# Values of a decoder's attention layer as seven block products between the heads, with two weight sums on GpSimd

## The chip, the core and the metric

The kernel runs on one core of one Trainium2 chip, in one launch. The metric is device time in microseconds of that core. TensorE (PE) multiplies, VectorE (DVE), ScalarE (ACT) and GpSimd (POOL) work element by element, SyncE (SP) issues most DMAs. Each engine takes its own instructions in the order of its program, and the engines meet at semaphores.

## The reference, cut to what matters

A two-layer decoder trunk on 256 tokens of width 1024, all in float32. Layer 0 is a recurrent block with a mixture of experts; layer 1 is causal attention with a mixture of experts. Keys and values come from the residual stream once, queries from the layer's input:

```python
h = layer_norm(xs, g, b)
kv = (h @ w_kv).reshape(B, S, 2, N_HEADS, HEAD_DIM)      # 256x1024 @ 1024x2048
k = apply_partial_rope(kv[:, :, 0], cos, sin)
v = kv[:, :, 1]
q = apply_partial_rope((x @ w_q).reshape(B, S, N_HEADS, HEAD_DIM), cos, sin) * (HEAD_DIM ** -0.5)
...                                                      # MOBA_BLOCK = SEQ = 256: plain causal attention
probs = jax.nn.softmax(s_own, axis=-1)                   # 8 heads of 128, 256 queries x 256 keys
out = probs @ v_own
return out.reshape(B, S, N_HEADS * HEAD_DIM) @ w_o
```

What matters here is v = h @ w_v, a product of 256x1024 by 1024x1024, and the eight heads that are worked on beside it.

## The kernel before, in words

The program is written out by hand for each engine, and a wait is a wait for a count of a semaphore. Layer 1's attention runs through these steps:

- Keys and queries (`keys0`, `query0`) are each formed as seven block products in place of eight: the tokens are split in two (c) and the inner and the output dimension in halves (j, h). The blocks are combined beforehand by four sums of weights (t1 to t4, each 128x2048) and four sums of operands (s1 to s4, each 128x512) on DVE, and afterwards by sums over the products in PSUM. `first_sum`, `second_sum`, `third_sum`, `fourth_sum` make t1 to t4, `kq_operands` makes s1, s2, s4, s3, `middle_products` and `kq_last` multiply, `middle_sums`, `seventh_sums` and `last_sum` combine. `sums_at` numbers all these sums on the one semaphore `sums`.
- `heads(c, b, count)` turns (transposes) a half of the tokens by heads behind `rope`; `heads_out` copies the result out of PSUM on ACT and DVE.
- Values are plain: `values_in(h, c, ks)` (L1043) multiplies one of four output blocks over eight chunks k, 32 products of 128x512, and `values_out` (L1316) copies a block to `vt` on ACT.
- Of head h, `head_scores(h)` (L1047) multiplies queries by keys; DVE takes the row maxima (L2028 to L2030, `negmax`); `exped(h)` on ACT (L1344) exponentiates; `probs(h)` on DVE (L2018) divides by the sum, in place in `prob`; `head_turn(h)` on PE (L1057) turns the probabilities; `turned(h)` on ACT (L1354) copies them to one of four places of `prT`; `head_values(h)` on PE (L1067) multiplies them by the values; `heads_done(j)` on ACT (L1360) copies two heads' output to `oT`.
- PE's order (L1078 to L1117) puts pieces of the values between the heads: two products of 128x512 stand between the scores of a head and the turning of the head before it. `head_values` 0 to 2 lie among them, 3 behind `head_turn(6)`, 4 to 7 behind `head_turn(7)`.
- DVE's order (L1985 to L2034): the sums of keys and queries, then `weight_sums(1)` (L1447: two sums of 128x2048 for the output projection `mix(1)`), the last `heads_out`, and then nothing but maxima and probabilities till the last head. After that `moe(1)` begins with `operand_sums(1)` for the output projection.
- `mix(1)` (L631) multiplies `oT` by the output weights, again with seven products; the routing and the experts follow. SP issues the loads of experts 3 and 5 of layer 1 when the values are multiplied (L546), that of expert 4 behind the last head (L549), those of experts 0 and 1 behind the output projection (L551), and in a loop the rest (`expert_loop`).
- GpSimd clears six small tiles at the start (L1397 to L1404) and does nothing else.

The line of most matmuls in the profile is that of the helper `mm`, L564; turning a half by heads is L670, turning probabilities L1064, all ACT operations L1125, sums over PSUM on DVE L1529.

Of the kernel before, what the change touches and what calls it, by code (L numbers as in the profile page):

```python
# [100 lines left out]
SEVEN = ("mix0", "pg0", "keys0", "query0", "mix1", "pg1")  # L101
# [4 lines left out]
FIRST_OUT = {"mix0": 1, "pg0": 2, "keys0": 5, "query0": 6, "mix1": 9, "pg1": 10}  # L106
# [7 lines left out]
FAR = 3e38  # L114

# [22 lines left out]
def build(nc, xt_d, x_d, pt_d, cst_d, cstb_d, chan_d, rows_d, tab_d, win_d, gates_d, wout_d, shared_d,  # L138
          router_d, experts_d, ple_d, pgate_d, wkv_d, wq_d, wo_d, out_d):
    ctx = ExitStack()  # L140
    with ctx:
# [97 lines left out]
        prT = z[:, :, :].rearrange("p c n -> p (c n)")[:, 0:4 * 3 * P].rearrange("p (b n) -> p b n", b=4)  # L239
# [114 lines left out]
        KQ_BANK = {"keys0": {"A": 0, "C": 1, "B": 2, "D": 3, "last": 2}, "query0": {"A": 4, "C": 5, "B": 6, "D": 7, "last": 6}}  # L354
        KQ_NAME = {"keys0": "wk", "query0": "wq"}
        KQ_MM = {"keys0": "k_mm", "query0": "q_mm"}
        KQ_SUM = {"keys0": (3, 11), "query0": (7, 11)}
        KQ_JOINT = {"keys0": joint, "query0": flat[:, 3 * D:3 * D + HALF]}

        def kq_lhs(stage, c, j):  # L360
            return {"keys0": hkT, "query0": xT}[stage][:, 4 * j:4 * j + 4, own(c)]
# [35 lines left out]
        def _(sp):  # L397
# [148 lines left out]
            sp.wait_ge(S("v_mm"), TC * 2)  # L546
# [15 lines left out]
        def _(pe):  # L562
# [7 lines left out]
            pe.wait_ge(S("pads0"), 1)  # L570
# [388 lines left out]
            def project(lhs, name, c, h, b, done, ks=range(KC)):  # L959

                for k in ks:
                    m = mm(bank(b), lhs[:, k, own(c)], kmajor(f"{name}{k // 2}")[:, k % 2, half(h)], k == 0, k == KC - 1)
                if KC - 1 in ks:
                    m.then_inc(S(done), 1)

# [25 lines left out]
            def middle_products(stage):  # L991
# [5 lines left out]
                kq_product(stage, "C", GSUM[0], kq_sum(stage, 0))  # L997
# [4 lines left out]
                kq_product(stage, "B", GSUM[1], kq_sum(stage, 1))  # L1002
                pe.wait_ge(S("first_out"), {"keys0": 7, "query0": 8}[stage])
                pe.wait_ge(S("sums"), sums_at[stage, "s4"])
                kq_product(stage, "C", GSUM[3], kq_weight(stage, 1, 1), False)
                pe.wait_ge(S("sums"), sums_at[stage, "t3"])
                pe.wait_ge(S("sums"), sums_at[stage, "s3"])
                kq_product(stage, "D", GSUM[2], kq_weight(stage, 0, 1))

            def kq_last(stage):  # L1010

                pe.wait_ge(S("sums"), sums_at[stage, "t4"])
                kq_product(stage, "last", kq_lhs(stage, 1, 1), kq_weight(stage, 0, 0))
# [29 lines left out]
            def values_in(h, c, ks):  # L1043

                project(hkT, "wv", c, h, 2 * h + c, "v_mm", ks)
# [21 lines left out]
            def head_values(h):  # L1067

                b, o = (h // 2) % 2, (h % 2) * T
                pe.wait_ge(S("v_out"), 2 if h < 4 else 4)  # L1070
# [3 lines left out]
                mm(PS[:, b, o:o + T], vt[:, 0, h * P:h * P + P], prT[:, h % 4, 0:T], True, False, True)  # L1074
                mm(PS[:, b, o + P:o + T], vt[:, 1, h * P:h * P + P], prT[:, h % 4, T:3 * P], False, True, True
                   ).then_inc(S("value_mm"), 1)
# [5 lines left out]
            values_in(0, 0, range(KC))  # L1082
            heads(1, 6, 8)
            values_in(0, 1, range(0, 2))
# [38 lines left out]
        def _(act):  # L1123
# [174 lines left out]
            def second_out(stage):  # L1298

                act.wait_ge(S(KQ_MM[stage]), 2)  # L1300
                out, src = tokm[:, 0, half(0)], PS[:, KQ_BANK[stage]["A"], :]
                if stage == "keys0":
                    out, src = out.rearrange("p (b t) -> p b t", b=2), PS[:, 0:2, 0:T]
                a(out, src, ACT.Copy).then_inc(S("copied"), 1)

            def third_out(stage):

                act.wait_ge(S(KQ_MM[stage]), 3)
                a(tokm[:, 1, half(1)], PS[:, KQ_BANK[stage]["C"], :], ACT.Copy).then_inc(S("first_out"), 1)

# [4 lines left out]

            def values_out(n, h, c):  # L1316

                act.wait_ge(S("v_mm"), n)
                a(vt[:, c, half(h)], PS[:, 2 * h + c, :], ACT.Copy).then_inc(S("v_out"), 1)
# [21 lines left out]
            values_out(1, 0, 0)  # L1341
# [12 lines left out]
            def turned(h):  # L1354
                act.wait_ge(S("probT_mm"), h + 1)
                if h >= 4:
                    act.wait_ge(S("value_mm"), h - 3)
                a(prT[:, h % 4, :], PS[:, 6 + h % 2, 0:3 * P], ACT.Copy).then_inc(S("probT_out"), 1)
# [6 lines left out]
            exped(0)  # L1365
            exped(1)
            turned(0)
            exped(2)
            values_out(2, 0, 1)
# [8 lines left out]
            values_out(3, 1, 0)  # L1378
            heads_done(0)
            turned(5)  # L1380
            exped(7)
            load_norm(2)
            turned(6)
# [11 lines left out]
        @block.gpsimd  # L1395
        def _(pool):
            nc.gpsimd.memset(z[:, 0, 0:T], 0.0).then_inc(S("pads0"), 1)  # L1397
            nc.gpsimd.memset(pads[:, :, 0:3], 0.0).then_inc(S("pads0"), 1)
            nc.gpsimd.memset(eps[:, :], LN_EPS).then_inc(S("pads0"), 1)
            nc.gpsimd.memset(onesr[:, :], 1.0).then_inc(S("pads0"), 1)  # L1400
            nc.gpsimd.memset(rankt[:, :, NOBLK:NCOL], -AWAY).then_inc(S("pads0"), 1)
            nc.gpsimd.memset(gtmp[:, :, 0, 4:NG], FAR).then_inc(S("pads0"), 1)
            pool.wait_ge(S("pads0"), 6)
            nc.gpsimd.memset(ovs[:, 2:4], 0.0).then_inc(zero_ok, 1)  # L1404


        @block.vector
        def _(dve):
# [439 lines left out]
            def kq_operands(stage, steps):  # L1848

                a11, a21, a12, a22 = (kq_lhs(stage, c, j) for j in range(2) for c in range(2))  # L1850
                for i in steps:
                    if i:
                        dve.wait_ge(S("sums"), sums_at[stage, ("s1", "s2")[min(i, 2) - 1]])
                    out, x, y, op = ((GSUM[0], a21, a22, ALU.add), (GSUM[1], GSUM[0], a11, ALU.subtract),
                                     (GSUM[3], a12, GSUM[1], ALU.subtract), (GSUM[2], a11, a21, ALU.subtract))[i]
# [103 lines left out]
            def middle_sums(stage):  # L1959

                dve.wait_ge(S(KQ_MM[stage]), 4)
                dve.wait_ge(S("first_out"), {"keys0": 7, "query0": 8}[stage])
                own_joint, banks = KQ_JOINT[stage], KQ_BANK[stage]
                step(added(own_joint, own_joint, PS[:, banks["B"], :]))
                step(added(tokm[:, 1, half(1)], tokm[:, 1, half(1)], own_joint))
                dve.wait_ge(S(KQ_MM[stage]), 5)
                step(added(tokm[:, 0, half(1)], own_joint, PS[:, banks["C"], :]))

            def seventh_sums(stage):

                dve.wait_ge(S(KQ_MM[stage]), 6)
                step(added(tokm[:, 1, half(1)], tokm[:, 1, half(1)], PS[:, KQ_BANK[stage]["D"], :]))
                step(added(tokm[:, 1, half(0)], KQ_JOINT[stage], PS[:, KQ_BANK[stage]["D"], :]))

            def last_sum(stage):

                dve.wait_ge(S(KQ_MM[stage]), KQ)
                step(added(tokm[:, 1, half(0)], tokm[:, 1, half(0)], PS[:, KQ_BANK[stage]["last"], :]))
# [36 lines left out]
            weight_sums(1)  # L2015
            heads_out(8, qT, 1, 7, "heads_dve")

# [7 lines left out]
            for i in range(NH + 1):  # L2025
# [5 lines left out]
                if i >= 1:  # L2031
                    probs(i - 1)
            n = moe(1)
# [115 lines left out]
```

## Time and profile before

| what | value |
|---|---|
| time, median of 3 runs | 1233.07 us (1232.51 to 1233.27) |
| the profiled execution | 1231.53 us, span 1229.7 us |
| PE busy | 1177.7 us, 96% of the span |
| DVE busy | 496.2 us, 40% |
| ACT busy | 260.5 us, 21% |
| POOL busy | 1.0 us |
| mean granted TensorE clock | 0.983 |

The profile's page has the busy time by engine, a strip of 40 slices, the chain of work that ended last, and the costliest groups of instructions. The trace behind it can be asked for the instructions of a stretch in order of time (the timeline), for busy time and granted clock by stretch (the windows), and for who waited for whom. All times in a stretch are microseconds from the start of the span. Spans of one timeline row overlap a little with the next, since the ends of matmuls are modelled: the time from start to start is what a group takes.

### The profile page before, as it was taken

To read this page: it belongs to the slowest core of one execution; us is meant where nothing else is said; L and a number is where in the kernel's file an instruction comes from. 1 tells how busy PE (TensorE), PEld (TensorE's weight loads), DVE (VectorE), ACT (ScalarE), POOL (GpSimd) and SP (SyncE) were. 2 spreads that over 40 slices of the span, in tenths; PEclk is the share of its full clock that TensorE was granted. 3 is DMA by queue.
4 is the path that set the end of the run, shared out by engine and by line. 5 is a ranking of instruction groups with operands and counts; after the bars stand their busy time and mean duration, and the time that the engine had idled before them with its cause. 6 is when DMAs were issued, how large, how long until landed. Compare 5 with 4: busy or idle time off the path is not lost.

```text
span 1229.7 us, 15413 instructions
## 1 busy us (share of the span) xinstructions
PE 1177.7 (96%) x5908; PEld 597.9 (49%) x5908; DVE 496.2 (40%) x1172; ACT 260.5 (21%) x471; POOL 1.0 (0%) x11
## 2 busy tenths in 40 slices
PE   9999997969999999999999999997599999999998
PEld 7866443425444444444645555442244444444344
DVE  4787432122222223226885383322122233223147
ACT  1513111101111112112412422120112111122112
POOL 0000000000000000000000000000000000000000
PEclk9999999979999999999999999998799999999999
DMA  9966999999999999999635478999999999999990
GB/s 379 400 244 284 403 420 419 427 425 428 424 425 426 424 426 425 419 421 421 274 137 205 165 321 339 414 417 424 426 425 426 425 424 425 425 424 423 421 401 36
DMA packets 50475, 461.65 MB, mean 375 GB/s; under 512 B 5729, under 2 KB 6242, under 8 KB 9186
## 3 DMA queue, kind: packets, MB, share of 16 engines
q1 hardware_dynamic: 48816, 456.09, 89.1%
q10 hardware_dynamic: 1586, 4.57, 1.0%
q8 instruction: 47, 0.77, 0.3%
q14 instruction: 26, 0.21, 0.0%
HBM read 459.60 MB, written 1.05 MB: 375 GB/s over the span
## 4 chain that ended last, share of the span: by engine, by line
PE 86%; DMA 8%; issue 3%; SPq 2%; DVE 1%; ACTq 0%; DVEq 0%
PE ps L564 82%; DMA weights<-in_experts 7%; SPq L406 2%; PE ps L670 1%; PE ps L843 1%; PE ps L850 1%; DMA xT<-in_xt 1%; SPq L409 1%; DVE x_lo L1611 0%; PE ps L1064 0%; SPq L456 0%; DVE x_res L1789 0%; DVE z L1788 0%; DVE onehot L1619 0%; DVE scratch L1699 0%
## 5 line engine op out<-in xcount | busy, mean ns | idle before, releaser
L564 PE MATMUL ps<-weights,xT 128*64 128x512 f32 (+2 forms) x1912 | 463.9, 605 | 43.0 <-issue 37.8
L564 PE MATMUL ps<-weights,scratch 128*64 128x512 f32 (+3 forms) x1192 | 328.1, 590 | 1.3 <-DVE scratch L1699 1.2
L564 PEld LDWEIGHTS ps<-weights,xT 128*64 128x64 f32 (+2 forms) x1912 | 151.7, 135 | 290.3 <-issue 277.9
L564 PEld LDWEIGHTS ps<-weights,scratch 128*64 128x64 f32 (+2 forms) x1192 | 114.4, 144 | 145.8 <-issue 143.5
L564 PE MATMUL ps<-scratch,xT 128*64 128x512 f32 (+2 forms) x384 | 158.1, 566 | 0.1
L1696 DVE TENSOR_TENSOR scratch<-scratch,ps 128x256 f32<-128x256 f32 x56 | 23.6, 421 | 314.1 <-ACT scratch L1125 314.1
L1709 DVE SCALAR_TENSOR_TENSOR y_lo<-ps,slot_weight,y_hi 128x512 fp32r<-128x512 f32 x112 | 84.0, 751 | 152.6 <-ACT y_hi L1125 152.6
L1125 ACT ACTIVATE y_hi<-ps,slot_weight 128x512 fp32r<-128x512 f32 x112 | 76.7, 687 | 251.6 <-PE ps L564 238.8
L1125 ACT ACTIVATE scratch<-ps 128x256 f32<-128x256 f32 (+2 forms) x75 | 30.5, 406 | 459.4 <-PE ps L564 442.4
L1125 ACT ACTIVATE xT<-ps 128x512 f32<-128x512 f32 x132 | 77.5, 598 | 97.9 <-PE ps L564 82.6
L564 PE MATMUL ps<-onehot,x_hi 128*128 128x256 f32 x448 | 91.1, 289 | 0.0
L564 PE MATMUL ps<-onehot,x_lo 128*128 128x256 f32 x448 | 89.0, 283 | 0.5 <-DVE x_lo L1611 0.3
L564 PEld LDWEIGHTS ps<-onehot,x_hi 128*128 128x128 f32 x448 | 69.8, 189 | 24.6 <-issue 21.3
L564 PE MATMUL ps<-y_hi,onehot_T 128*128 128x512 f32 x224 | 80.6, 438 | 0.0
L564 PE MATMUL ps<-scratch 128*64 128x512 f32 (+1 forms) x160 | 72.8, 598 | 0.0
L564 PEld LDWEIGHTS ps<-scratch,xT 128*64 128x64 f32 (+2 forms) x384 | 49.6, 143 | 47.0 <-issue 45.1
L1699 DVE COPY scratch<-ps 128x256 f32<-128x256 f32 x56 | 23.8, 425 | 120.5 <-PE ps L843 120.5
L564 PE MATMUL ps<-y_lo,onehot_T 128*128 128x512 f32 x224 | 70.8, 394 | 0.0
L564 PEld LDWEIGHTS ps<-onehot,x_lo 128*128 128x128 f32 x448 | 68.8, 190 | 1.3 <-DVE x_lo L1611 1.3
L564 PE MATMUL ps<-xT,weights 128*128 128x256 f32 x256 | 56.4, 380 | 1.6 <-DMA xT<-in_xt 1.5
L564 PEld LDWEIGHTS ps<-xT,weights 128*128 128x128 f32 x256 | 48.4, 190 | 9.3 <-DMA xT<-in_xt 2.8
L564 PEld LDWEIGHTS ps<-y_hi,onehot_T 128*128 128x128 f32 x224 | 34.5, 190 | 25.5 <-issue 23.7
(210 smaller groups left out, 769.7 us busy)
## 6 DMA issues: line engine op xcount, KB each, us to landing
weights<-in_experts SPq DMA_DIRECT2D x90, 2048.0 KB, 19.4
weights<-in_experts SPq DMA_DIRECT2D x140, 1024.0 KB, 24.4
scratch<-in_experts SPq DMA_DIRECT2D x18, 2048.0 KB, 20.9
scratch<-in_experts SPq DMA_DIRECT2D x24, 1024.0 KB, 22.0
weights<-in_pgate SPq DMA_DIRECT2D x8, 1024.0 KB, 27.2
weights<-in_wkv SPq DMA_DIRECT2D x8, 1024.0 KB, 26.2
weights<-in_win SPq DMA_DIRECT2D x7, 1024.0 KB, 20.0
weights<-in_shared SPq DMA_DIRECT2D x6, 1024.0 KB, 10.4
```

Of the source, the lines that this page charges most:

```text
L406: sp.dma_start(E(SLOT_OF[p])[:, ks], src[:, ks]).then_inc(S(f"{GATE_UP[part]}{p // 2 % 4}_loaded_{L}"), 16)
L409: sp.dma_start(E(SLOT_OF[p])[:, GU:EXPERT], src[:, GU:EXPERT]).then_inc(S(f"down{p // 2 % 4}_loaded_{L}"), 16)
L564: return nc.tensor.matmul(out, lhsT, rhs, start=first, stop=last, skip_group_check=shared_bank)
L670: m = nc.tensor.transpose(PS[:, b + j, k * P:k * P + P], src[:, c, (4 * j + k) * P:(4 * j + k + 1) * P], ident)
L843: m = nc.tensor.transpose(PS[:, 6, f * P:f * P + P], hh[:, f * P:f * P + P], ident)
L850: m = nc.tensor.transpose(PS[:, 7, (2 + c) * P:(3 + c) * P], ohw[:, c, :], ident)
L1125: return nc.scalar.activation(out, in_, f, **kw)
L1696: v.tensor_tensor(hh, sg, PS[:, 6, DE:2 * DE], ALU.mult).then_inc(S(f"hidden_{L}"), 1)
L1699: v.tensor_copy(hT.rearrange("p f s -> p (f s)"), PS[:, 6, 0:DE]).then_inc(S(f"hidT_{L}"), 1)
L1709: v.scalar_tensor_tensor(y_lo[:, half(h)], PS[:, 4 + h, :], wslot[:, 0:1], y_hi[:, half(h)].bitcast(F32), ALU.mult, ALU.subtract).then_inc ...
```

## The change

- Values become a third stage, `value0`, of the seven block products: 28 products of 128x512 in place of 32. The first of them is `value_part` (two halves into one bank), then `first_sum_product`, `second_sum_product`, `fourth_sum_product`, `third_sum_product`, `kq_last`, one each between the scores of one head and the turning of the head before.
- `value0` needs four sums of weights. t1 and t2 are made on DVE, t1 where `weight_sums(1)` was, t2 behind the last `heads_out` and two operand sums. t3 and t4 are made on GpSimd, which waits for t1, and for t2 and the first product. t1 waits for all of `query0`'s products, since it is written over query weights.
- The operand sums s1 and s2 stand on DVE behind the last `heads_out`, s4 and s3 behind head 0's maxima; the sums over the products (`middle_sums`, `seventh_sums`, `last_sum`) behind the probabilities of heads 2, 3 and 4. Two of the four output blocks are copied on ACT (`second_out`, `third_out`), the other two are written by DVE.
- `head_values` moves: 0 and 1 behind `head_scores(6)`, with no product between, 2 behind `head_scores(7)`, 3 to 5 behind `head_turn(6)`, 6 and 7 behind `head_turn(7)`. `prT` has five places in place of four. On ACT, `heads_done(0)` and `heads_done(1)` stand behind `turned(6)`.
- `weight_sums(1)` moves behind the last probabilities. The router weights' load on ACT's queue moves ahead of `turned(6)`. SP's load of experts 3 and 5 waits for the seventh product.

```diff
+HEADS_AHEAD = 5
...
+                   "value0": {"A": 0, "C": 1, "B": 2, "D": 3, "last": 2}}
+        KQ_SUM = {"keys0": (3, 11), "query0": (7, 11), "value0": (0, 1)}
+        VSUM = [xT[:, 2 * i:2 * i + 2, :].rearrange("p k s -> p (k s)").rearrange("p (k s) -> p k s", k=4) for i in range(4)]
...
-            sp.wait_ge(S("v_mm"), TC * 2)
+            sp.wait_ge(S("v_mm"), KQ)
...
+            def third_sum_product(stage):
+
+                if stage == "value0":
+                    pe.wait_ge(S("pool_sums"), 7)
+                else:
+                    pe.wait_ge(S("sums"), sums_at[stage, "t3"])
                 pe.wait_ge(S("sums"), sums_at[stage, "s3"])
...
-            values_in(0, 0, range(KC))
+            value_part(0, range(4))
             heads(1, 6, 8)
-            values_in(0, 1, range(0, 2))
+            pe.wait_ge(S("first_out"), FIRST_OUT["value0"])
+            value_part(1, range(0, 2))
...
             head_scores(0)
-            values_in(0, 1, range(2, 4))
+            value_part(1, range(2, 4))
             head_scores(1)
-            values_in(0, 1, range(4, 6))
+            first_sum_product("value0")
             head_turn(0)
             head_scores(2)
-            values_in(0, 1, range(6, 8))
+            second_sum_product("value0")
             head_turn(1)
             head_scores(3)
-            values_in(1, 0, range(0, 2))
+            fourth_sum_product("value0")
             head_turn(2)
             head_scores(4)
-            values_in(1, 0, range(2, 4))
+            third_sum_product("value0")
             head_turn(3)
             head_scores(5)
-            head_values(0)
-            values_in(1, 0, range(4, 6))
+            kq_last("value0")
             head_turn(4)
             head_scores(6)
+            head_values(0)
             head_values(1)
-            values_in(1, 0, range(6, 8))
             head_turn(5)
             head_scores(7)
             head_values(2)
-            values_in(1, 1, range(0, 4))
             head_turn(6)
-            values_in(1, 1, range(4, 8))
             head_values(3)
+            head_values(4)
+            head_values(5)
             head_turn(7)
-            for h in range(4, NH):
-                head_values(h)
+            head_values(6)
+            head_values(7)
...
             exped(0)
+            second_out("value0")
             exped(1)
+            third_out("value0")
             turned(0)
...
-            values_out(4, 1, 1)
-            act.dma_start(routw, router_d).then_inc(S("router_loaded"), 16)
+            heads_done(0)
+            heads_done(1)
             turned(7)
-            for j in range(1, 4):
-                heads_done(j)
+            heads_done(2)
+            heads_done(3)
...
+            for i in range(4):
+                arrived(pool, f"wv{i}")
+            pool.wait_ge(S("sums"), sums_at["value0", "t1"])
+            nc.gpsimd.tensor_tensor(kq_weight("value0", 0, 1), kq_weight("value0", 1, 1), kq_weight("value0", 0, 1), ALU.subtract
+                                    ).then_inc(S("pool_sums"), 1)
+            pool.wait_ge(S("v_mm"), 1)
+            pool.wait_ge(S("sums"), sums_at["value0", "t2"])
+            nc.gpsimd.tensor_tensor(kq_weight("value0", 0, 0), kq_weight("value0", 1, 0), kq_sum("value0", 1), ALU.subtract
+                                    ).then_inc(S("pool_sums"), 1)
...
             rope(7, 1, 0)
-            weight_sums(1)
+            first_sum("value0")
             heads_out(8, qT, 1, 7, "heads_dve")
+            kq_operands("value0", range(0, 2))
+            second_sum("value0")
...
                 if i >= 1:
                     probs(i - 1)
+                if i == 0:
+                    kq_operands("value0", range(2, 4))
+                elif i == 3:
+                    middle_sums("value0")
+                elif i == 4:
+                    seventh_sums("value0")
+                elif i == 5:
+                    last_sum("value0")
+            weight_sums(1)
             n = moe(1)
```

## Rows read from the trace of the kernel before

**Rows 1.** The page: busy us, share of the span, instructions, by engine.

```profile
PE 1177.7 (96%) x5908; PEld 597.9 (49%) x5908; DVE 496.2 (40%) x1172; ACT 260.5 (21%) x471; POOL 1.0 (0%) x11
```

**Rows 2.** Windows: stretch, its length, busy us by engine, clock, DMA.

```profile
665.00:700.00 35.00, 35.00 (x151) 21.39 (x151) 11.38 (x48) 15.24 (x48) 0.00 (x0) 1.00 0.18 61
700.00:735.00 35.00, 34.97 (x130) 19.49 (x129) 28.09 (x71) 10.25 (x16) 0.00 (x0) 1.00 0.81 336
```

**Rows 3.** Timeline of PE, values and heads: start, us, engine, line, operation.

```profile
656.21 7.03 PE L564 MATMUL ps<-weights,scratch 128*128 128x512 f32 x16
663.08 1.04 PE L670 MATMUL ps<-cst,z 128*128 128x128 f32 x8
...
672.03 1.94 PE L564 MATMUL ps<-weights,scratch 128*128 128x512 f32 x4
673.80 0.51 PE L1064 MATMUL ps<-cst,scratch 128*128 128x128 f32 x3
674.14 0.39 PE L564 MATMUL ps<-scratch,lnp 128*128 128x128 f32 x2
...
674.97 1.94 PE L564 MATMUL ps<-weights,scratch 128*128 128x512 f32 x4
...
688.01 0.87 PE L564 MATMUL ps<-z,scratch 128*128 128x256 f32 x4
688.72 3.60 PE L564 MATMUL ps<-weights,scratch 128*128 128x512 f32 x8
692.15 0.49 PE L1064 MATMUL ps<-cst,scratch 128*128 128x128 f32 x3
...
696.90 2.87 PE L564 MATMUL ps<-z,scratch 128*128 128x256 f32 x16
699.60 3.60 PE L564 MATMUL ps<-weights,xT 128*128 128x512 f32 x8
```

**Rows 4.** Timeline of DVE, the same stretch.

```profile
636.31 0.69 DVE L1856 TENSOR_TENSOR scratch<-scratch,xT 128x512 f32<-128x512 f32 x1
...
657.94 2.29 DVE L1453 TENSOR_TENSOR weights<-weights 128x2048 f32<-128x2048 f32 x1
...
664.15 0.69 DVE L1983 COPY lnp<-ps 128x512 f32<-128x512 f32 x1 [1.50 <-PE ps L670]
...
672.23 0.29 DVE L2028 TENSOR_REDUCE wgtt<-ps 128x1 f32<-128x128 f32 x1 [1.46 <-PE ps L564]
...
673.16 0.29 DVE L2021 TENSOR_SCALAR scratch<-scratch,wgtt 128x128 f32<-128x128 f32 x1
673.36 0.35 DVE L2022 TENSOR_SCALAR scratch<-scratch,wgtt 128x256 f32<-128x256 f32 x1
...
700.43 0.69 DVE L1529 TENSOR_TENSOR scratch<-xT 128x512 f32<-128x512 f32 x1 [9.66 <-ACT xT L1125]
```

**Rows 5.** Timeline of ACT, the last turned head and two heads' output.

```profile
697.10 0.49 ACT L1125 ACTIVATE z<-ps 128x384 f32<-128x384 f32 x1 [0.38 <-PE ps L1064]
697.48 0.59 ACT L1125 ACTIVATE xT<-ps 128x512 f32<-128x512 f32 x1
```

**Rows 6.** Timeline of POOL, its two longest instructions of eleven.

```profile
0.71 0.31 POOL L1397 MEMSET z<- 128x256 f32 x1 [0.29 <-POOLq L2139]
...
1.04 0.26 POOL L1400 MEMSET ones_row<- 128x192 f32 x1
```

**Rows 7.** Timeline of PE behind its longest idle time.

```profile
882.84 1.07 PE L564 MATMUL ps<-weights,xT 128*32 128x512 f32 x2 [12.59 <-issue]
...
888.78 0.59 PE L564 MATMUL ps<-scratch,xT 128*32 128x512 f32 x1
...
889.21 0.59 PE L564 MATMUL ps<-scratch,xT 128*32 128x512 f32 x1
```

**Rows 8.** Windows over and behind that idle time, columns as in rows 2.

```profile
870.00:883.00 13.00, 0.41 (x6) 0.19 (x8) 2.44 (x10) 0.69 (x1) 0.00 (x0) 0.70 1.00 425
883.00:886.00 3.00, 3.00 (x16) 0.71 (x15) 0.00 (x0) 0.00 (x0) 0.00 (x0) 0.50 1.04 437
```

**Rows 9.** Timeline of SP: loads of experts around the output projection.

```profile
724.73 0.33 SPq L402 DMA_DIRECT2D weights<-in_experts  x1
...
742.76 2.52 SPq L406 DMA_DIRECT2D weights<-in_experts  x4
```

More of the change, by code:

```diff
@@ L353, in build @@
         KQ = 7
[L354 to L358, printed above, removed]
+        KQ_BANK = {"keys0": {"A": 0, "C": 1, "B": 2, "D": 3, "last": 2}, "query0": {"A": 4, "C": 5, "B": 6, "D": 7, "last": 6},
+                   "value0": {"A": 0, "C": 1, "B": 2, "D": 3, "last": 2}}
+        KQ_NAME = {"keys0": "wk", "query0": "wq", "value0": "wv"}
+        KQ_MM = {"keys0": "k_mm", "query0": "q_mm", "value0": "v_mm"}
+        KQ_SUM = {"keys0": (3, 11), "query0": (7, 11), "value0": (0, 1)}
+        KQ_JOINT = {"keys0": joint, "query0": flat[:, 3 * D:3 * D + HALF], "value0": joint}
+        KQ_OUT = {"keys0": tokm, "query0": tokm, "value0": vt}
+        VSUM = [xT[:, 2 * i:2 * i + 2, :].rearrange("p k s -> p (k s)").rearrange("p (k s) -> p k s", k=4) for i in range(4)]
+        KQ_OPERANDS = {"keys0": GSUM, "query0": GSUM, "value0": VSUM}
         def kq_lhs(stage, c, j):
-            return {"keys0": hkT, "query0": xT}[stage][:, 4 * j:4 * j + 4, own(c)]
+            return {"keys0": hkT, "query0": xT, "value0": hkT}[stage][:, 4 * j:4 * j + 4, own(c)]
         def kq_weight(stage, j, h):
@@ L956, in _ @@
             after(0)
[L959 to L964, printed above, removed]
             def heads(c, b, count):
@@ L1041, in _, with value_part @@
             kq_last("query0")
-            def values_in(h, c, ks):
-                project(hkT, "wv", c, h, 2 * h + c, "v_mm", ks)
+            def value_part(j, ks):
+                for k in ks:
+                    m = mm(bank(KQ_BANK["value0"]["A"]), kq_lhs("value0", 0, j)[:, k, :], kq_weight("value0", j, 0)[:, k // 2, k % 2, :],
+                           j == 0 and k == 0, k == 3, j == 1)
+                if 3 in ks:
+                    m.then_inc(S("v_mm"), 1)
             def head_scores(h):
@@ L1069, in head_values @@
                 b, o = (h // 2) % 2, (h % 2) * T
-                pe.wait_ge(S("v_out"), 2 if h < 4 else 4)
+                pe.wait_ge(S("v_out"), 2)
                 pe.wait_ge(S("probT_out"), h + 1)
@@ L1300, in second_out @@
                 act.wait_ge(S(KQ_MM[stage]), 2)
-                out, src = tokm[:, 0, half(0)], PS[:, KQ_BANK[stage]["A"], :]
+                out, src = KQ_OUT[stage][:, 0, half(0)], PS[:, KQ_BANK[stage]["A"], :]
                 if stage == "keys0":
                     out, src = out.rearrange("p (b t) -> p b t", b=2), PS[:, 0:2, 0:T]
-                a(out, src, ACT.Copy).then_inc(S("copied"), 1)
+                a(out, src, ACT.Copy).then_inc(S("v_out" if stage == "value0" else "copied"), 1)
             def third_out(stage):
                 act.wait_ge(S(KQ_MM[stage]), 3)
-                a(tokm[:, 1, half(1)], PS[:, KQ_BANK[stage]["C"], :], ACT.Copy).then_inc(S("first_out"), 1)
+                a(KQ_OUT[stage][:, 1, half(1)], PS[:, KQ_BANK[stage]["C"], :], ACT.Copy).then_inc(S("first_out"), 1)
             def heads_out(n, dst, c, b, done):
@@ L1355, in turned @@
                 act.wait_ge(S("probT_mm"), h + 1)
-                if h >= 4:
-                    act.wait_ge(S("value_mm"), h - 3)
-                a(prT[:, h % 4, :], PS[:, 6 + h % 2, 0:3 * P], ACT.Copy).then_inc(S("probT_out"), 1)
+                if h >= HEADS_AHEAD:
+                    act.wait_ge(S("value_mm"), h - HEADS_AHEAD + 1)
+                a(prT[:, h % HEADS_AHEAD, :], PS[:, 6 + h % 2, 0:3 * P], ACT.Copy).then_inc(S("probT_out"), 1)
             def heads_done(j):
@@ L1377, in _ @@
             exped(6)
-            values_out(3, 1, 0)
-            heads_done(0)
             turned(5)
@@ L1853, in kq_operands @@
                         dve.wait_ge(S("sums"), sums_at[stage, ("s1", "s2")[min(i, 2) - 1]])
-                    out, x, y, op = ((GSUM[0], a21, a22, ALU.add), (GSUM[1], GSUM[0], a11, ALU.subtract),
-                                     (GSUM[3], a12, GSUM[1], ALU.subtract), (GSUM[2], a11, a21, ALU.subtract))[i]
+                    sums = KQ_OPERANDS[stage]
+                    out, x, y, op = ((sums[0], a21, a22, ALU.add), (sums[1], sums[0], a11, ALU.subtract),
+                                     (sums[3], a12, sums[1], ALU.subtract), (sums[2], a11, a21, ALU.subtract))[i]
                     v.tensor_tensor(out, x, y, op).then_inc(S("sums"), 1)
@@ L1961, in middle_sums @@
                 dve.wait_ge(S(KQ_MM[stage]), 4)
-                dve.wait_ge(S("first_out"), {"keys0": 7, "query0": 8}[stage])
+                dve.wait_ge(S("first_out"), THIRD_OUT[stage])
                 own_joint, banks = KQ_JOINT[stage], KQ_BANK[stage]
                 step(added(own_joint, own_joint, PS[:, banks["B"], :]))
-                step(added(tokm[:, 1, half(1)], tokm[:, 1, half(1)], own_joint))
+                step(added(KQ_OUT[stage][:, 1, half(1)], KQ_OUT[stage][:, 1, half(1)], own_joint))
                 dve.wait_ge(S(KQ_MM[stage]), 5)
-                step(added(tokm[:, 0, half(1)], own_joint, PS[:, banks["C"], :]))
+                step(added(KQ_OUT[stage][:, 0, half(1)], own_joint, PS[:, banks["C"], :]))
             def seventh_sums(stage):
                 dve.wait_ge(S(KQ_MM[stage]), 6)
-                step(added(tokm[:, 1, half(1)], tokm[:, 1, half(1)], PS[:, KQ_BANK[stage]["D"], :]))
-                step(added(tokm[:, 1, half(0)], KQ_JOINT[stage], PS[:, KQ_BANK[stage]["D"], :]))
+                step(added(KQ_OUT[stage][:, 1, half(1)], KQ_OUT[stage][:, 1, half(1)], PS[:, KQ_BANK[stage]["D"], :]))
+                step(added(KQ_OUT[stage][:, 1, half(0)], KQ_JOINT[stage], PS[:, KQ_BANK[stage]["D"], :]))
             def last_sum(stage):
                 dve.wait_ge(S(KQ_MM[stage]), KQ)
-                step(added(tokm[:, 1, half(0)], tokm[:, 1, half(0)], PS[:, KQ_BANK[stage]["last"], :]))
+                ins = added(KQ_OUT[stage][:, 1, half(0)], KQ_OUT[stage][:, 1, half(0)], PS[:, KQ_BANK[stage]["last"], :])
+                if stage == "value0":
+                    ins.then_inc(S("v_out"), 1)
+                else:
+                    step(ins)
             def heads_out(n, dst, c, b, done):
```

62 lines of the change are left out of this document (36 added, 26 removed), and 3 rows, old and new, of the table SUM_ORDER.

## The prediction

> **What bounds the kernel now.** I read the page's shares first: PE is busy 96% of the span, DVE 40%, POOL not at all [rows 1]. Then the windows of the stretch that the change touches, 665 to 700 and on to 735: PE busy 35.00 of 35.00 us and 34.97 of 35.00, at full granted clock, DVE busy 11.38 us and DMA at 0.18 in the first [rows 2]. So PE's own list sets the time there, and anything that makes PE stand still is added one for one. Last I read the timelines of PE, DVE and ACT, to see how far ahead of PE each waited-for step is done [rows 3 to 5]. That distance is small: the scores of a head are through at 672.03, the turning of the head before starts at 673.80, 1.77 us later [rows 3]. Two products in between take 1.72 us, so 0.05 us is already waited for.
>
> Does a shift of PE at 700 reach the end? The experts' stream is bound by DMA (PE stands still while the DMA share is 1.00, [rows 8]), but it is started by PE: experts 0 and 1 are issued at 724.73, behind the output projection, and the first of the loop at 742.76 [rows 9]. Both move with PE. The earlier issue of experts 3 and 5 only fills a stretch in which DMA waits for PE anyway. I pass shifts on in full.
>
> **Removed.** A product of 128x512 is two instructions, and 16 instructions take 663.08 - 656.21 = 6.87 us, 0.429 us each [rows 3]. 28 products in place of 32 take away eight: **-3.44 us**. The four waits of 0.05 us in front of head_turn(0) to (3) go as well, since a whole product block (3.43 us) now stands where 1.72 us stood: **-0.2 us**.
>
> **The tail of the heads.** From the scores to the turned head a path of 1.77 us must pass: 0.20 us until DVE starts at 672.23, maxima and probabilities until 673.36 + 0.35 = 673.71, 0.09 us until PE starts [rows 3, 4]. What stands beside it now?
> - head_turn(5) stands behind head_scores(6) and two head_values. One of these takes 688.72 - 688.01 = 0.71 us [rows 3], two 1.42: PE waits **0.35 us**.
> - head_turn(6) stands behind head_scores(7) and one head_values: 1.77 - 0.71 = **1.06 us**.
> - head_values(4) needs heads_done(0), which ACT now does behind turned(6). After the turning: 0.20 us until ACT starts, turned 0.38 us until the next, the copy 0.59 (start to start, and length, [rows 5]), 0.1 until PE: 1.3 to 1.4 us, of which head_values(3) covers 0.71: **0.66 us**.
> - head_turn(7) is far enough back. head_values(7) no longer stands behind three others (in the before four take 2.70 us, [rows 3]), but its copy is covered by head_values(6) up to about **0.1 us**.
>
> Together +2.2 us. With the two terms above the change stands at 2.2 - 3.44 - 0.2 = **-1.5 us** if nothing else stops PE.
>
> **DVE's new work, by itself.** The head of the list, replayed from rows: t1 657.94 to 660.23 (as before), PE is done with the first block at 656.21 + 3.44 and with the turning 0.87 us later at 660.5, heads_out from 660.7, s1 from 661.3 (0.69 us and 0.04 of link each, [rows 4]), s2 from 662.1, t2 from 662.7 to 665.0, the maxima of head 0 from 664.9 although its scores are there at 663.1, s4 and s3 0.6 us each, probabilities of head 0 done at 668.4. PE reaches head_turn(0) at 669.1, behind its third block. Nothing is late; the slack is **0.6 us**. Later heads have 3.44 us beside a path of 1.77, against at most two or three extra sums of 0.73 us, which fall where DVE waited (middle_sums and seventh_sums wait for PE's blocks, and the maxima queued behind them are late by at most 0.3 us). weight_sums(1) took the slot from 657.94; now it runs behind the last probabilities in DVE's idle 9.66 us before 700.43 [rows 4], and is done about when heads_done(3) is. The output projection's second product needs it 3.4 us after the first starts: cost nothing. If that cover were gone, each would cost 2.29 us.
>
> **GpSimd's two sums.** No row of the trace shows such an instruction, nor GpSimd and DVE at work together. Its length g: at least DVE's 2.29 us for the same shape [rows 4]; from above, its memsets grow by 0.05 us from 192 to 256 elements, 0.8 us per 1000 [rows 6], and a sum touches 3 x 2048 elements: 5.1 us. Two accesses instead of three would be 3.4. I take 4.3, the middle of the last two, being GpSimd's own rows. PE wants t3 behind its sixth block, near 680, and t4 20 us later than t2: their length costs PE nothing directly. What they do to DVE is the open cost. Below, zero: both work undisturbed. Above: a DVE operation that uses SBUF on both inputs, or runs at two elements a cycle (tensor_scalar, 0.06 us more for 128 more elements, [rows 4]), stands until the GpSimd instruction is through.
>
> In that case: GpSimd starts t3 at 660.3, DVE's s1 stands from 661.3 to 660.3 + g. t2 follows 3.7 us later and ends at 664.0 + g. At once GpSimd starts t4, and after the maxima of head 0 DVE stands again, until 664.1 + 2g. Behind this are queued s4, s3, the maxima of head 1 and the probabilities of head 0, 2.8 us, and on PE head_turn(0) with everything after it: it starts at 667.0 + 2g in place of 669.1. PE's wait is **2g - 2.1 us**: 6.5 us at g = 4.3, 2.5 at 2.3, 8.1 at 5.1. The change as a whole is then 2g - 3.6, zero at g = 1.8.
>
> I take the upper end of this cost, at g = 4.3: **+6.5 us**, sum **+5.0 us**. The rows by themselves don't decide between the ends; I hold that two engines reading four streams of SBUF at once exclude each other to be likelier than that they don't.
>
> The Trainium skill speaks against this change here. "SBUF — State Buffer", section "SBUF: two separate sides", says that DVE and GpSimd take turns at a shared pair of ports, as an exclusive lock held for a whole instruction, for DVE operations with two SBUF inputs among others; by it the wait is the full one, and without it the change would be -1.5 us. "GPSIMD Engine Reference", section "3.1 Elementwise — side-by-side cycle accounting", gives 4497 ns for a sum of 2048 float32 elements beside 2293 ns on DVE; the trace agrees on DVE's (2.29 us), no row shows GpSimd's, and with it the sum, as an estimate, would be 5.4 in place of 5.0 us.
>
> **The clock.** With 6.5 us of standing, PE's clock may fall. Over its idle 12.59 us before 882.84 the granted clock averages 0.70, and it is 0.50 (1.2 GHz) in the 3 us behind it [rows 7, 8]. From 882.84 to 888.78 seven rounds of four matmuls take 5.94 us; the next takes 0.43 [rows 7], so 5.94 - 7 x 0.43 = 2.9 us were lost. No row shows a wait as short as ours: between 0 and 2.9 us. Of the rows with any fall this is the only kind, and I take **+2.9 us**.
>
> **Sum.** -3.44 - 0.2 + 2.2 + 6.5 + 2.9 = +7.9 us on the profiled span of 1229.7: 1237.6, an execution of 1239.5. The profiled execution (1231.53) is 1.5 us below the median, and I add the difference to the median: **1241.0 us**.
>
> **Rivals.**
> - Full block, as above: 1236.5 to 1243.5, according to g and the clock. Chance 0.58.
> - No contention: DVE runs at full rate beside GpSimd, PE waits only in the tail: 1231.6 us. For it: nothing in the rows forbids it. Chance 0.22; 0.03 of it below 1230.6.
> - Partial contention: DVE's operations are stretched, not stopped, and half of the block's delay is seen: 1233.1 - 1.5 + 3.3 = 1234.9. It decides at the 0.6 us of slack in front of head_turn(0). Chance 0.12, half of it over 1235.5.
> - **The other side:** no contention, and the tail's waits are not there either, because PE's turning starts earlier than I think behind an idle PE and ACT finds time for heads_done(0) before turned(6) is due. Place: head_turn(6), whose path would have to be 0.71 us instead of 1.77. 1233.1 - 3.6 = 1229.4. Against it: the path of 1.77 us appears four times in the trace. Chance 0.05.
> - weight_sums(1), now behind the last probabilities, is stopped too or late and delays the output projection by one sum and more: 1243 and up. Chance 0.03.
>
> This kernel's measurement can tell about 0.2%, 2.5 us, from no change. Faster (below 1230.6): 0.08; within: 0.25; slower (above 1235.5): 0.67. Range 1230.8 to 1243.5: it takes in the case without contention down to its middle's lower side, and leaves out some 0.17.
>
> **What would show it.** After: PE busy without a gap up to the third block of values, then an idle time of 2g - 2.1 us before L1064's first turning, released by DVE; on DVE gaps before s1 and before s4 that end with a POOL instruction; on POOL two instructions of 4 to 5 us; a granted clock of 0.5 behind the gap; waits of 0.35, 1.06 and 0.66 us in the tail. 56 instructions of value products. What would make it wrong: s1 starting at 661.3 beside a running GpSimd, or GpSimd's sums far shorter or longer than 4.3 us.

## The result and the profile after

The changed kernel takes 1239.77 us (median of 4 runs, 1238.01 to 1241.21), the kernel before 1232.79 us (4 runs, 1232.05 to 1233.27). The ratio is 1.0064, 95% interval 1.005 to 1.0077: slower by 7.0 us. The profiled execution took 1239.84 us, its span is 1238.0 us. Forecast were 1241.0 us in a range of 1230.8 to 1243.5.

The page's first lines and part of its strip, kernel after; they answer to [rows 1]:

```profile
span 1238.0 us, 15424 instructions
PE 1175.7 (95%) x5900; PEld 597.5 (48%) x5900; DVE 514.2 (42%) x1184; ACT 259.7 (21%) x470; POOL 10.0 (1%) x13
PEclk9999998979999999999998999998799999999999
```

PE is busy 2.0 us less, and the kernel is slower all the same. POOL has 9 us of work that it did not have. The timeline of PE, kernel after (start, us, engine, line, operation, and in brackets the idle time and what ended it), answers to [rows 3]:

```profile
666.37 3.65 PE L571 MATMUL ps<-weights,xT 128*128 128x512 f32 x8
676.33 0.90 PE L1090 MATMUL ps<-cst,scratch 128*128 128x128 f32 x3 [6.30 <-DVE scratch L2063]
...
682.76 0.49 PE L1090 MATMUL ps<-cst,scratch 128*128 128x128 f32 x3
...
697.83 1.53 PE L571 MATMUL ps<-z,scratch 128*128 128x256 f32 x8
699.56 0.55 PE L1090 MATMUL ps<-cst,scratch 128*128 128x128 f32 x3 [0.21 <-DVE scratch L2063]
...
700.77 0.87 PE L571 MATMUL ps<-z,scratch 128*128 128x256 f32 x4
702.51 0.55 PE L1090 MATMUL ps<-cst,scratch 128*128 128x128 f32 x3 [0.86 <-DVE scratch L2063]
702.89 0.82 PE L571 MATMUL ps<-z,scratch 128*128 128x256 f32 x4
704.22 1.55 PE L571 MATMUL ps<-z,scratch 128*128 128x256 f32 x8 [0.51 <-ACT xT L1151]
...
707.49 3.60 PE L571 MATMUL ps<-weights,xT 128*128 128x512 f32 x8
```

The third block of values begins at 666.37 and takes eight instructions of 0.429 us, to 669.80. The first turning (L1090, the line that was L1064) starts at 676.33: 6.53 us of standing. Three small waits follow in the tail. The timelines of POOL and DVE, kernel after, show whom PE waits for, and answer to [rows 4] and [rows 6]:

```profile
661.03 4.51 POOL L1431 TENSOR_TENSOR weights<-weights 128x2048 f32<-128x2048 f32 x1 [659.50 <-DVE weights L1857]
669.17 4.49 POOL L1435 TENSOR_TENSOR weights<-weights 128x2048 f32<-128x2048 f32 x1 [3.62 <-DVE weights L1867]
```

```profile
661.36 0.69 DVE L2022 COPY lnp<-ps 128x512 f32<-128x512 f32 x1 [0.49 <-PE ps L677]
661.97 4.13 DVE L1891 TENSOR_TENSOR xT<-scratch 128x512 f32<-128x512 f32 x1
666.13 0.69 DVE L1891 TENSOR_TENSOR xT<-xT,scratch 128x512 f32<-128x512 f32 x1
...
669.14 0.41 DVE L2070 TENSOR_REDUCE wgtt<-ps 128x1 f32<-128x256 f32 x1
669.59 4.10 DVE L2071 TENSOR_SCALAR wgtt<-wgtt 128x2 f32<-128x2 f32 x1
```

The sum s1 is a 128x512 operation like its neighbour s2 of 0.69 us, but its record lasts 4.13; the scaling of two numbers a row, 0.17 us for every other head, lasts 4.10. Less their own length both end 0.13 us before GpSimd's record does (665.41 and 665.54, 673.52 and 673.66). Two instructions that read PSUM run at their usual length beside GpSimd: the copy at 661.36 (0.69 us) and the second of head 0's maxima at 669.14 (0.41 us). The stopped time shows as busy in DVE's row of the page, so its share says nothing of it.

### The profile page after: what moved, and what is told of

Read it like the earlier page. It is cut to its first block, busy times and chain, and to the rows that moved or that the text cites. A ratio compares the mean times of both kernels' runs of the same rounds, so it can differ in the third digit from the quotient of the medians.

```text
span 1238.0 us, 15424 instructions
## 1 busy us (share of the span) xinstructions
PE 1175.7 (95%) x5900; PEld 597.5 (48%) x5900; DVE 514.2 (42%) x1184; ACT 259.7 (21%) x470; POOL 10.0 (1%) x13
## 4 chain that ended last, share of the span: by engine, by line
PE 81%; DMA 9%; SPq 4%; issue 4%; DVE 2%; ACT 0%; ACTq 0%; DVEq 0%
PE ps L571 77%; DMA weights<-in_experts 9%; SPq L413 3%; PE ps L677 1%; PE ps L850 1%; PE ps L857 1%; SPq L416 1%; DMA xT<-in_xt 0%; DVE xT L1891 0%; DVE wgtt L2071 0%; DVE x_lo L1643 0%; PE ps L1090 0%; DVE weights L1867 0%; SPq L463 0%; DVE x_res L1821 0%
## 5 line engine op out<-in xcount | busy, mean ns | idle before, releaser
L571 PE MATMUL ps<-weights,xT 128*64 128x512 f32 (+2 forms) x1944 | 478.5, 603 | 45.3 <-issue 39.8
L571 PE MATMUL ps<-weights,scratch 128*64 128x512 f32 (+3 forms) x1152 | 309.7, 590 | 1.3 <-DVE scratch L1731 1.2
L571 PEld LDWEIGHTS ps<-weights,xT 128*64 128x64 f32 (+2 forms) x1944 | 157.6, 136 | 298.6 <-issue 283.9
L571 PEld LDWEIGHTS ps<-weights,scratch 128*64 128x64 f32 (+2 forms) x1152 | 107.3, 142 | 139.3 <-issue 137.3
L571 PEld LDWEIGHTS ps<-y_lo,onehot_T 128*128 128x128 f32 x224 | 42.0, 188 | 10.1 <-issue 0.5
```

The source lines that it names most:

```text
L571: return nc.tensor.matmul(out, lhsT, rhs, start=first, stop=last, skip_group_check=shared_bank)
```

## The experiments

The theory: a running GpSimd sum stops DVE's next instruction that needs SBUF twice, for as long as it runs; PE waits what exceeds the slack; the tail's waits come from the new order alone. The rivals: DVE's longer list by itself makes PE wait; or the tail's waits are a consequence of the delay at the head. Medians are given with the ratio to the kernel before, run on the same chip.

**e1: all sums on DVE.**

```diff
-            nc.gpsimd.tensor_tensor(kq_weight("value0", 0, 1), kq_weight("value0", 1, 1), kq_weight("value0", 0, 1), ALU.subtract
-                                    ).then_inc(S("pool_sums"), 1)
...
-            nc.gpsimd.tensor_tensor(kq_weight("value0", 0, 0), kq_weight("value0", 1, 0), kq_sum("value0", 1), ALU.subtract
-                                    ).then_inc(S("pool_sums"), 1)
...
+                elif i == 1:
+                    third_sum("value0")
+                elif i == 2:
+                    fourth_sum("value0")
                 elif i == 3:
                     middle_sums("value0")
```

> The changed kernel with t3 and t4 made by DVE (behind the probabilities of heads 0 and 1) instead of GpSimd; all else as changed. Theory (GpSimd's sums hold DVE up): DVE's s1 runs right behind heads_out(8), the 6.5 us of PE standing before head_turn(0) and the half clock behind it are gone, the tail's waits of 0.3, 1.0 and 0.6 us stay; 1.5 us faster than the kernel before, about 1231.4 us. Rival (the longer list of DVE alone, t2 ahead of head 0's maxima, makes PE wait): with two more sums of 2.3 us on DVE it is no faster than the changed kernel, 1239 us or more.

1231.39 us (11 runs), ratio 0.9992, interval 0.9983 to 1.0001. PE's timeline, e1: the standing time is gone, 665.69 + 3.43 = 669.12 to 669.18.

```profile
665.69 3.65 PE L571 MATMUL ps<-weights,xT 128*128 128x512 f32 x8
669.18 0.49 PE L1084 MATMUL ps<-cst,scratch 128*128 128x128 f32 x3
...
673.82 0.38 PE L1084 MATMUL ps<-cst,scratch 128*128 128x128 f32 x2
...
690.62 0.55 PE L1084 MATMUL ps<-cst,scratch 128*128 128x128 f32 x3 [0.21 <-DVE scratch L2048]
693.56 0.55 PE L1084 MATMUL ps<-cst,scratch 128*128 128x128 f32 x3 [0.86 <-DVE scratch L2048]
695.27 1.55 PE L571 MATMUL ps<-z,scratch 128*128 128x256 f32 x8 [0.51 <-ACT xT L1145]
...
698.54 3.60 PE L571 MATMUL ps<-weights,xT 128*128 128x512 f32 x8
```

The interval takes in 1, so e1 is not told apart from the kernel before. DVE has 4.6 us more work than in the changed kernel, and the median is 8.4 us lower: the longer list is not the cause. The three waits of the tail are the same to the hundredth, so they do not come from the delay at the head.

**e2: e1, and another order in the tail.** `last_part` is the last product, one half at a time.

```diff
-            kq_last("value0")
+            last_part(range(0, 2))
             head_turn(4)
             head_scores(6)
-            head_values(0)
-            head_values(1)
+            last_part(range(2, 4))
             head_turn(5)
             head_scores(7)
+            head_values(0)
+            head_values(1)
             head_values(2)
             head_turn(6)
...
-            turned(6)
             heads_done(0)
+            turned(6)
...
-                elif i == 5:
+                elif i == 6:
                     last_sum("value0")
```

> As e1, and the tail put in another order: the last product in two halves in front of head_turn(4) and head_turn(5), head_values 0 to 2 in front of head_turn(6), heads_done(0) ahead of turned(6), last_sum one head later. Theory (the tail's waits are the 1.77 us path with too little beside it): waits of 0.05 us at head_turn(4) and (5), none at head_turn(6) and head_values(4); the whole saving of four products is left, 3.4 us faster than before, about 1229.4 us. Rival (the tail's waits move to the next place, since DVE or ACT is late in sum): the waits appear at other turnings and the time stays at e1's 1231.4 us.

1229.36 us (9 runs), ratio 0.9978, interval 0.9968 to 0.9988: faster than both kernels, and 3.0 us below the kernel before on the same chip (1232.34), where 3.4 had been expected. PE's timeline, e2, has no bracket left in the stretch:

```profile
683.03 1.94 PE L571 MATMUL ps<-weights,scratch 128*128 128x512 f32 x4
685.06 0.55 PE L1094 MATMUL ps<-cst,scratch 128*128 128x128 f32 x3
...
689.21 2.18 PE L571 MATMUL ps<-z,scratch 128*128 128x256 f32 x12
...
695.41 3.60 PE L571 MATMUL ps<-weights,xT 128*128 128x512 f32 x8
```

From e1 to e2 the stretch from the first block of values to the output projection shrinks from 698.54 - 656.17 = 42.37 us to 695.41 - 654.95 = 40.46, by 1.91; the medians differ by 2.03. Where e2 misses its forecast: head_turn(4) starts 2.03 us behind 683.03, not 1.77. DVE's timeline shows why: the two sums of `seventh_sums` (1.41 us, from 682.08) end at 683.5, and the maxima of head 5, ready at 683.2, stand behind them. So 0.26 us of waiting are left there. No bracket shows them, since the modelled end of the products (683.03 + 1.94 = 684.97) lies only 0.09 us ahead of the turning.

**e3: t3 on GpSimd, t4 on DVE** (e1's edit for t4 alone).

> The changed kernel with t3 on GpSimd and t4 on DVE. Theory (each GpSimd sum stops DVE once, for its own length): s1 stands until GpSimd's 4.5 us are over, 3.5 us late, 0.6 of it is slack: PE waits 2.9 us in front of head_turn(0); the change is +1.4 us against before, 1234.2 us, up to 1236 if the clock falls. If what stopped DVE was something else than the running GpSimd instruction, PE's wait stays near 6.5 us.

1234.80 us (7 runs), ratio 1.0023, interval 1.0011 to 1.0035. PE's timeline, e3:

```profile
666.68 3.65 PE L571 MATMUL ps<-weights,xT 128*128 128x512 f32 x8
672.71 0.55 PE L1087 MATMUL ps<-cst,scratch 128*128 128x128 f32 x3 [2.38 <-DVE scratch L2056]
```

From 666.68 + 3.43 = 670.11 to 672.71 are 2.60 us. s1's record is 4.13 us again (3.44 too many), the scaling's 0.17. The wait is 0.3 us shorter than expected.

**e4: both GpSimd sums over half of their columns.** t3 and t4 are formed for the first 256 of 512 columns only, so the kernel does not compute the reference's values.

```diff
...
-            nc.gpsimd.tensor_tensor(kq_weight("value0", 0, 0), kq_weight("value0", 1, 0), kq_sum("value0", 1), ALU.subtract
+            nc.gpsimd.tensor_tensor(kq_weight("value0", 0, 0)[:, :, :, 0:T], kq_weight("value0", 1, 0)[:, :, :, 0:T], kq_sum("value0", 1)[:, :, :, 0:T], ALU.subtract
```

> The changed kernel with both GpSimd sums over half of their columns (128x1024), so the values are not the reference's. Theory (the wait is twice the sum's length less 2.1 us): sums of 2.3 us, PE waits 2.5 to 3 us in front of head_turn(0), +1.2 us against before, 1234.0 us, more by up to 1.8 if the clock falls. If the wait does not depend on the length, it stays at 6.5 us and the time at 1239.8.

1234.37 us (10 runs), ratio 1.0019, interval 1.001 to 1.0029. GpSimd's records, then DVE's two, then PE's turning, e4:

```profile
660.64 2.35 POOL L1431 TENSOR_TENSOR weights<-weights 128x1024 f32<-128x1024 f32 x1 [659.10 <-DVE weights L1857]
666.61 2.34 POOL L1435 TENSOR_TENSOR weights<-weights 128x1024 f32<-128x1024 f32 x1 [3.62 <-DVE weights L1867]
```

```profile
661.57 1.97 DVE L1891 TENSOR_TENSOR xT<-scratch 128x512 f32<-128x512 f32 x1
667.03 1.95 DVE L2071 TENSOR_SCALAR wgtt<-wgtt 128x2 f32<-128x2 f32 x1
```

```profile
665.97 3.65 PE L571 MATMUL ps<-weights,xT 128*128 128x512 f32 x8
671.62 0.55 PE L1090 MATMUL ps<-cst,scratch 128*128 128x128 f32 x3 [1.99 <-DVE scratch L2063]
```

One account fits the three kernels. Take what DVE's two records have too much, less a slack of 0.84 us:

| kernel | s1 | scaling | sum less 0.84 | PE stood |
|---|---|---|---|---|
| after | 4.13 - 0.69 = 3.44 | 4.10 - 0.17 = 3.93 | 6.53 | 6.53 |
| e3 | 3.44 | 0 | 2.60 | 2.60 |
| e4 | 1.97 - 0.69 = 1.28 | 1.95 - 0.17 = 1.78 | 2.22 | 671.62 - 669.40 = 2.22 |

The slack was fitted on the first row and then holds for the other two, also where the expectations of e3 and e4 (2.9 and 2.5 to 3 us) lay above, mainly since they took 0.6 us of slack. e1 gives it without a fit: DVE's probabilities of head 0 end at 668.22 and PE comes at 669.12, 0.90 us later, of which 0.06 is the way from DVE's end to PE's start (676.27 to 676.33 in the changed kernel).

**e5: e2's tail with GpSimd's sums kept.**

> The changed kernel, GpSimd's sums kept, with e2's order of the tail alone. Theory (head and tail wait separately and add): PE's 6.5 us before head_turn(0) and the half clock stay, the tail's waits go; 2.0 us less than the changed kernel, 1237.8 us, 1.0045 of before. If the tail's waits came from the delay at the head, nothing is gained: 1239.8 us.

1237.01 us (5 runs), ratio 1.0036, interval 1.0022 to 1.005. Its one wait with a bracket is the head's:

```profile
665.09 3.65 PE L571 MATMUL ps<-weights,xT 128*128 128x512 f32 x8
...
675.05 0.90 PE L1100 MATMUL ps<-cst,scratch 128*128 128x128 f32 x3 [6.31 <-DVE scratch L2074]
```

675.05 - 668.52 = 6.53 us again, and in the tail only the 0.26 us in front of head_turn(4) that e2 has too. Head and tail add: from the third block to the output projection are 707.49 - 666.37 = 41.12 us after and 704.10 - 665.09 = 39.01 in e5, 2.11 less. Of these 0.19 lie between the first turning and the second (6.43 us after, 681.29 - 675.05 = 6.24 in e5), behind the standing and at the lower clock. That leaves 1.92 us for the tail with GpSimd's sums, beside e2's 1.91 without.

**The exclusion by itself.** Three kernels add one GpSimd instruction on buffers that nobody reads any more to the kernel before, p1 a sum, p2 a copy, p3 a memset, all 128x2048, started by the scores of head 3. SP's loads of experts 3 and 5 wait for it as well:

```diff
+            pool.wait_ge(S("q_mm"), KQ)
+            pool.wait_ge(S("score_mm"), 4)
+            nc.gpsimd.tensor_tensor(W[:, 0, :], W[:, 0, :], W[:, 1, :], ALU.subtract).then_inc(S("probed"), 1)
```

> The kernel before, with one GpSimd tensor_tensor of 128x2048 float32 on two weight buffers that nobody reads any more, started when the scores of head 3 are through. Theory (exclusion): the first DVE instruction with SBUF in and out after it, the scaling of the maxima, stands until GpSimd is done, 4.5 - 0.45 us; PE waits 4.0 us in front of head_turn(2), 1236.8 us, up to 2 more for the clock. No exclusion: DVE's records keep their length, 1232.8 us.

> As p1 with a GpSimd tensor_copy (one input) of the same shape. If any GpSimd instruction that reads SBUF excludes DVE's two-port instructions, PE waits the copy's length less 0.45 us: 1.3 to 2 us at 1.7 to 2.4 us of length. If only two inputs do, nothing changes: 1232.8 us.

> As p1 with a GpSimd memset of 128x2048 (no input), 1.7 us long by the memsets' slope. If writing alone is enough to exclude DVE, PE waits 1.2 us, 1234.0 us; if only reading counts, nothing, 1232.8 us.

One execution each, 1238.26, 1232.59 and 1234.44 us (before beside them 1230.43), so their times decide little: the 28 executions of the kernel before that stand beside e1 reach from 1229.4 to 1234.3 us. The records decide. For p1, p2 and p3 in this order, GpSimd's instruction and DVE's scaling of the maxima:

```profile
674.94 4.50 POOL L1408 TENSOR_TENSOR weights<-weights 128x2048 f32<-128x2048 f32 x1 [673.41 <-PE ps L565]
675.48 3.98 DVE L2034 TENSOR_SCALAR wgtt<-wgtt 128x2 f32<-128x2 f32 x1
```

```profile
675.26 1.89 POOL L1408 COPY weights<-weights 128x2048 f32<-128x2048 f32 x1 [673.73 <-PE ps L565]
675.81 1.37 DVE L2034 TENSOR_SCALAR wgtt<-wgtt 128x2 f32<-128x2 f32 x1
```

```profile
675.86 1.80 POOL L1408 MEMSET weights<- 128x2048 f32 x1 [674.33 <-PE ps L565]
676.43 1.26 DVE L2034 TENSOR_SCALAR wgtt<-wgtt 128x2 f32<-128x2 f32 x1
676.51 1.19 DVE L2024 RECIPROCAL wgtt<-wgtt 128x2 f32<-128x2 f32 x1
```

Each scaling ends within 0.1 us of GpSimd's instruction. PE's wait in front of head_turn(2) was 3.8, 1.2 and 1.0 us (4.0, 1.3 to 2 and 1.2 were expected). All three hold it up, the memset too, which reads nothing. They do it in two ways. Beside the sum and the copy DVE's next instruction (the reciprocal) starts about 0.08 us before the scaling's end, at 679.38 and 677.09. Beside the memset it starts 0.08 us behind the scaling's start, as it does undisturbed (672.88 and 672.96 in the kernel before), and both are held only at their ends, to 677.69 and 677.70.

Does the same hold for a DVE sum with two inputs from SBUF? p4 and p5 are e1 with a memset and with a copy on GpSimd, started by t1, so that they run when DVE comes to s1.

> e1 (all sums on DVE) with one GpSimd memset of 128x2048 on a dead buffer, started by t1, so that it runs when DVE comes to s1, a tensor_tensor with two SBUF inputs. If a GpSimd instruction that only writes stops this DVE instruction too, s1's record grows from 0.69 us to about 1.6 us (until the memset's 1.8 us are over); if only reading counts for it, s1 stays 0.69 us. PE's time hardly moves in either case (0.6 us of slack).

> As p4 with a GpSimd tensor_copy of 1.9 us (one input). A GpSimd instruction that reads SBUF stops a DVE instruction with two SBUF inputs: s1's record grows to about 1.7 us. If it took two reads on both sides, s1 stays 0.69 us.

GpSimd's instruction and s1, p4 and p5:

```profile
661.91 1.81 POOL L1423 MEMSET weights<- 128x2048 f32 x1 [660.38 <-DVE weights L1845]
662.89 0.68 DVE L1879 TENSOR_TENSOR xT<-scratch 128x512 f32<-128x512 f32 x1
```

```profile
660.30 1.89 POOL L1423 COPY weights<-weights 128x2048 f32<-128x2048 f32 x1 [658.77 <-DVE weights L1845]
661.26 1.48 DVE L1879 TENSOR_TENSOR xT<-scratch 128x512 f32<-128x512 f32 x1
```

Beside the memset s1 runs undisturbed, from 662.89 to 663.57 of a memset that lasts to 663.72; beside the copy it is stopped until about the copy's end (1.48 us in place of 0.68). The Trainium skill states this rule in "SBUF — State Buffer", section "SBUF: two separate sides": the pair of ports is taken by DVE operations in a 2-port mode, or by those with two SBUF inputs, the latter only against a GpSimd operation that reads SBUF. All five pairs of records agree with it, if the scaling is an operation in a 2-port mode; no record names the mode.

## Why the prediction was right, point by point

The first block of values starts 0.64 us later in the trace of after than before (656.85, 656.21). Start of the output projection less that: 43.39 us before, 50.64 after, 7.25 us more. Its parts, as forecast and as measured:

| step | forecast | measured |
|---|---|---|
| four products fewer | -3.44 | -3.44 (8 instructions fewer, 0.429 us each) |
| small waits of 0.05 us gone | -0.2 | 0: they were no waits (below); from a block's start to the turning behind it are still 3.49 us in e1 and e2, not 3.43 |
| PE's standing at head_turn(0) | +6.5 | +6.53 |
| half clock behind it | +2.9 | +1.8 |
| head_turn(5), head_turn(6) | +0.35, +1.06 | 1.73 - 1.42 = +0.31, 1.74 - 0.71 = +1.03 |
| head_values(4), (7) | +0.66, +0.1 | 1.33 - 0.71 = +0.62, 1.56 - 1.42 = +0.14 |
| sum | +7.9 | +7.0; 0.27 of the 7.25 is spread over the heads |

**The block's length.** GpSimd's sum takes 4.5 us where 4.3 was taken from the memsets' slope; the 4497 ns of the Trainium skill ("GPSIMD Engine Reference", section "3.1 Elementwise — side-by-side cycle accounting") were the better source. With half the columns it takes 2.35 us (e4). That the slope came so near is luck: it counts accesses, and by it two accesses of 2048 elements would take 3.4 us, where the copy, which has two, takes 1.89 (p2). By 2g - 2.1 a sum of 4.5 us would be 6.9 us of standing. That it is 6.53 comes from three small terms: the slack in front of head_turn(0) is 0.84 us and not 0.6 (-0.2), DVE goes on 0.13 us before each of GpSimd's records ends (-0.3), and GpSimd starts 0.17 us behind t1 (660.86 to 661.03) and 0.15 behind t2, where 0.1 was taken (+0.1). So the agreement of 6.5 and 6.53 is luck too; the mechanism is not. Its sign was forecast otherwise: not gaps in front of s1 and s4, but two records that grow, those of s1 and of the scaling of head 0's maxima.

**The clock** is the term that is off by most. The windows over the stretch, kernel after (columns as in [rows 2]), answer to [rows 8]:

```profile
669.80:676.33 6.53, 0.23 (x2) 0.01 (x1) 6.40 (x9) 2.08 (x8) 3.86 (x1) 0.75 0.00 0
676.33:682.76 6.43, 6.43 (x17) 3.74 (x18) 1.41 (x6) 2.12 (x8) 0.00 (x0) 0.72 0.00 0
```

The cycle from the first turning to the second takes 6.43 us; in e1, at full clock, 673.82 - 669.18 = 4.64. So 1.79 us were lost where 2.9 had been taken whole from the row behind an idle time of 12.6 us. e5 has the same wait and loses 6.24 - 4.64 = 1.60. The clock had fallen while PE still stood (0.75 on average, above), was 0.50 (1.2 GHz) from 676.33 to 678.62 and 1.00 again from 680.00. The row behind an idle time twice as long did not give this cost; here it was above it.

**The tail** was forecast to 0.04 us in each wait. From a head's scores to the turning of the head before a path over DVE's queue takes 1.73 to 1.74 us where PE waits for it, and whatever stands beside it can be counted; e2 and e5 show it by filling it.

**The four waits of 0.05 us** are the step that was misread. In the kernel before, two products behind a head's scores take 1.77 us even where no turning follows and DVE is not waited for:

```profile
666.49 1.94 PE L564 MATMUL ps<-weights,scratch 128*128 128x512 f32 x4
668.26 0.38 PE L564 MATMUL ps<-scratch,lnp 128*128 128x128 f32 x2
```

Behind a `head_values` they take 1.72 (681.56 to 683.28). So the 0.05 us belongs to products that follow scores, and stays with them in the changed kernel.

**The rest of the way** keeps the shift. From the output projection's start to the end of the span are 530.1 us before, 530.5 after, 531.0 in e1, 529.4 in e2. Experts 3 and 5 are issued at 687.93 in e1, 8 us earlier than before, without any gain: the next issues stand at 723.67, 1.1 us earlier than in [rows 9], as PE does.

**The rivals.** No contention would have given e1's 1231.4 us (1231.6 was forecast for it), and partial contention a shorter record of s1; both fell. weight_sums(1) was not stopped: GpSimd was long done.

What stays open is small. The medians of e3 and e4 stand 3.4 and 3.0 us above e1's, their traces explain 2.60 and 2.22. The 0.8 us between is less than the half width of each ratio's interval (1.1 to 1.5 us), so the medians do not tell it from nothing. What in the scores costs the products behind them 0.05 us is not known.

## What to carry to other kernels

A second engine is only free if it shares nothing with the first: put work on GpSimd where DVE reads PSUM, not where its SBUF instructions lie on the path. Price each GpSimd instruction at its whole length, less what DVE does before it is stopped and less the slack: here two of 4.5 us stopped DVE for 3.44 and 3.93 us and PE for 6.53, for 4.6 us of DVE work that had room in DVE's own list. When work is taken out of a bound engine's list, look at what it stood beside: products between the heads were also what hid a path of 1.74 us, and four of them fewer (3.44 us) brought nothing that could be told from the noise in e1, and 3.0 us once the rest was spread over the turnings (e2).

## What the runs showed of the hardware

- GpSimd: a float32 sum of 128x2048 takes 4.5 us, of 128x1024 2.35, a copy of 128x2048 1.89, a memset 1.80. A sum costs 2.4 times a copy.
- A DVE instruction that is stopped by GpSimd is recorded as busy for the whole time. An instruction on two numbers a row with a length of 4.1 us is such a stop.
- A GpSimd memset holds up the end of DVE's SBUF-to-SBUF scaling (1.26 us in place of 0.17) but not DVE's sum with two SBUF inputs (0.68 us). DVE's next instruction still started 0.08 us behind the scaling's start; beside a GpSimd sum or copy it started 3.90 or 1.28 us behind it.
- DVE instructions that read PSUM kept their length beside a GpSimd sum: a copy 0.69 us, a maximum 0.41 us.
- TensorE's clock may fall after the wait is over: in p1, PE stood for 3.8 us, turned at 680.17 with a granted clock of 1.00, and the four instructions from 681.38 took 3.20 us in place of 1.77, at 0.55. In the changed kernel, where PE stood for 6.53 us, it fell during the wait. After waits of 2.60 us (e3) and 2.22 us (e4) the granted clock stayed 1.00. PE's timeline, p1:

```profile
680.17 0.55 PE L1065 MATMUL ps<-cst,scratch 128*128 128x128 f32 x3 [3.61 <-DVE scratch L2026]
...
681.38 3.41 PE L565 MATMUL ps<-weights,scratch 128*128 128x512 f32 x4
684.58 0.75 PE L1065 MATMUL ps<-cst,scratch 128*128 128x128 f32 x3
```
